# Who makes the low halves of the weights: VectorE alone up to the first squared-ReLU MLP, VectorE and GpSimd from there on

## The chip, the core and the metric

The kernel runs on one core of a Trainium2 chip. The metric is the device time of one execution in microseconds (us). TensorE, VectorE, ScalarE and GpSimd each work through a list of instructions of their own in order, SyncE issues the loads, and semaphores hold them together. In the profile they are called PE (its weight loads PEld), DVE, ACT, POOL and SP.

## What is computed

Two transformer blocks in float32, batch 1, 512 tokens, width 1024, one after the other. What matters here is the order of the weight products:

```
first block
  proj = rmsnorm(x) @ w_in                 # q, k, v of two attentions, forget gates
  forgetting attention, 8 heads; stick-breaking attention, 8 heads
  x += concat(rmsnorm(fox_o), rmsnorm(sb_o)) @ w_out
  x += memory attention(rmsnorm(x), rmsnorm(mem); w_mq, w_mkv) @ w_mo
  u  = depthwise causal conv, width 3 (rmsnorm(x) @ w_up)     # 2 x 2816 columns
  x += (silu(gate) * val) @ w_down
second block
  z = gelu(rmsnorm(x) @ a_w_in);  u, v = split(z);  v = layernorm(v)
  x += (u * (W_s v + b)) @ a_w_out          # gated unit, 8 groups
  x += square(relu(rmsnorm(x) @ w1_0)) @ w2_0
  x += latent attention(rmsnorm(x)) @ b_w_o
  x += square(relu(rmsnorm(x) @ w1_1)) @ w2_1
  out = rmsnorm(x)
```

## The kernel before

Every large product is made of three matmuls in a reduced float32 format: both operands are split into a high half and a low half (the rest), and high x high, high x low and low x high are summed in a bank of TensorE's output memory, PSUM (split_sum, L374 to L385).

**The weight stream.** The weights come in 168 chunks of 128 x 2048 elements (1 MB), in the order in which TensorE uses them. weight_stream (L60) lists them; an item "tiles" in that list is no chunk, it only counts output tiles. 90 chunks stand ahead of the first call of mlp (L118), 78 from there on. raw, w_hi and w_lo have two slots each, so chunk c goes where chunk c-2 was. A chunk is split in PIECES = 2 halves j. SyncE loads chunk c into raw when chunk c-2 has been split (L308 to L312). ScalarE makes both halves of w_hi, a copy that rounds (split_high, L1447 to L1458), when TensorE has finished with chunk c-2. For w_lo = raw - w_hi, VectorE makes half 0 (split_low, L779 to L788), GpSimd makes half 1 (L350 to L353). TensorE waits for both before it uses the chunk (wait_chunk, L361).

**Where the halves stand in the order.** GpSimd has nothing else to do after its constants, so its half starts when ScalarE's second half is ready. VectorE's half is a place in its program: split_low() stands between the things that it does at each stage, and ScalarE has split_high() in the matching places. In the attentions the two halves of a chunk are split at two different steps of the loop (FOX_PIECES, SB_PIECES, MEM_PIECES, L268 and L269). VectorE's call for half 1 there issues nothing.

**What goes on around it.** TensorE writes output tiles to four banks in turn (next_bank, L365) and takes a bank again when VectorE has emptied the tile four before it (take, L790). VectorE empties back projections with L846, x += bank. In the conv MLP of the first block the unit is a granule of 256 up columns for gate and for value: TensorE does two chunks of up projection (by_feature), and one chunk of back projection (back, L419) of the granule before. VectorE takes four up tiles (L1109) with split_low after the second and the fourth, then runs gated_and_back (L1144): the convolution with L1120 and L1126, the products L1136, the low halves g_lo (L802), and between them the eight L846, and split_low at the end. Granules 1 to 10 run so; granule 0 has no back tiles beside it. In the gated unit VectorE does per group the biases (L1243), two takes (L1248), two products (L1256), two g_lo (L802) and eight L846, then split_low.

Of the kernel before, what the change touches and what calls it, by code (L numbers as in the profile page):

```python
# [35 lines left out]
PIECES = 2  # L36
# [23 lines left out]
def weight_stream(w):  # L60

    def columns(name, first, n=COLS, tiles=2):
        v = w[name].rearrange("(k p) n -> p k n", p=P)
        def parts(raw):
            return [(raw.rearrange("p (k n) -> p k n", n=COLS)[:, :, 0:n], v[:, :, first:first + n])]
        return SLOT, tiles, parts, max(n, P)

    def rows(name, granule):
        v = w[name].rearrange("(k p) n -> p k n", p=P)
        def parts(raw):  # L70
            return [(raw.rearrange("p (k n) -> p k n", k=2), v[:, 2 * granule:2 * granule + 2, :])]
        return SLOT, KT, parts, 0

    def k_rope(raw):
        v = w["kv_w_a_2"].rearrange("(k p) n -> p k n", p=P)
        d = raw.rearrange("p (k n) -> p k n", n=COLS)
        a, b = v[:, :, KV_LORA:KV_LORA + 32], v[:, :, KV_LORA + 32:KV_LORA + 64]
        return [(d[:, :, 0:32], a), (d[:, :, 32:64], b), (d[:, :, 64:96], b), (d[:, :, 96:128], a)]

    def q_heads(pair):  # L80

        v = w["b_w_q_b_2"].rearrange("(k p) n -> p k n", p=P)
        def parts(raw):
            d = raw[:, 0:3 * 512].rearrange("p (k n) -> p k n", n=512)
            out = []
            for j in range(2):
                at = (2 * pair + j) * (NOPE + ROPE)
                out += [(d[:, :, 256 * j:256 * j + 192], v[:, :, at:at + 192]),
                        (d[:, :, 256 * j + 192:256 * j + 224], v[:, :, at + 160:at + 192]),
                        (d[:, :, 256 * j + 224:256 * j + 256], v[:, :, at + 128:at + 160])]  # L90
            return out
        return 3 * 512, 4, parts, 0

    def kv_heads(c):
        v = w["kv_w_b_2"].rearrange("(k p) n -> p k n", p=P)
        return SLOT, 8, lambda raw: [(raw.rearrange("p (k n) -> p k n", k=2), v[:, :, 1024 * c:1024 * c + 1024])], 0

    def mlp(up, down):
        u = lambda g: columns(up, COLS * g)
        d = lambda g: rows(down, g)  # L100
        return [u(0), u(1)] + [x for i in range(14) for x in (d(i), u(2 + i))] + [d(14), d(15)]

    g = lambda n: columns("w_up", COLS * n)
    v = lambda n: columns("w_up", D_FF + COLS * n)
    d = lambda n: rows("w_down", n)
    w_in = lambda kind, n=2: [columns("w_in", HEADS * HD * kind + COLS * c) for c in range(n)]
    mkv = lambda *cs: [columns("w_mkv", COLS * c, tiles=2 if c < 4 else 1) for c in cs]
    out = [("tiles", KT)] + w_in(0) + [("tiles", KT), columns("w_in", 6 * HEADS * HD, n=HEADS, tiles=1)]
    out += w_in(1) + w_in(2) + mkv(0, 1, 2, 3) + w_in(3) + w_in(4) + w_in(5) + mkv(4, 5, 6)
    out += [rows("w_out", c) for c in range(2)] + mkv(7) + [rows("w_out", c) for c in range(2, 4)]  # L110
    out += [columns("w_mq", COLS * c) for c in range(4)] + [rows("w_mo", c) for c in range(4)]
    out += [g(0), v(0), g(1), v(1)] + [x for i in range(9) for x in (d(i), g(2 + i), v(2 + i))] + [d(9), d(10)]
    gate_v, gate_u = ([columns("a_w_in_2", at + COLS * c) for c in range(8)] for at in (GATE, 0))
    out += gate_v[0:6] + [("tiles", 2)] + gate_v[6:8] + [("tiles", 2)]
    out += gate_u[0:7] + [("tiles", 2)] + gate_u[7:8]
    for c in range(8):
        out += [("tiles", 2)] * (c < 7) + [rows("a_w_out_2", c)]
    out += mlp("w1_0", "w2_0")  # L118
    out += [columns("b_w_q_a_2", 0), columns("b_w_q_a_2", 256, n=128, tiles=1)]
    out += [columns("kv_w_a_2", 0), (SLOT, 1, k_rope, P)]  # L120
    out += [q_heads(p) for p in range(4)] + [kv_heads(c) for c in range(2)]
    out += [rows("b_w_o_2", c) for c in range(4)]
    out += mlp("w1_1", "w2_1")
    return out


def build(nc, w, out):
# [5 lines left out]
    with ExitStack() as ctx:  # L133
# [83 lines left out]
        w_split = sem("w_split")  # L217
# [56 lines left out]

        CHUNKS, ENDS, LOADS = [], [], []
        passed, loads = 0, [0, 0]
        for item in weight_stream(w):
            passed += item[1]
            if item[0] != "tiles":
                loads[len(CHUNKS) % 2] += 16 * len(item[2](raw[:, 0, :]))  # L280
                LOADS.append(loads[len(CHUNKS) % 2])
                CHUNKS.append(item)
                ENDS.append(passed)

        def split_piece(c, j):

# [10 lines left out]
        @block.sync  # L297
        def _(sp):
            x_cols = x_in.rearrange("(t p) n -> p t n", p=P)

            for c, (_, _, parts, _) in enumerate(CHUNKS):
                if c == 1:
                    for q in range(4):
                        sp.dma_start(x_stage[:, :, 256 * q:256 * q + 256], x_cols[:, :, 256 * q:256 * q + 256])\
                          .then_inc(x_loaded[q], 16)
                if c == 2:
                    sp.dma_start(mem_stage, mem_in.rearrange("(t p) n -> p t n", p=P)).then_inc(mem_loaded, 16)
                if c >= 2:  # L308
                    sp.wait_ge(w_split, c - 1)
                    sp.wait_ge(w_split_pool, c - 1)  # L310
                for dst, src in parts(raw[:, c % 2, :]):
                    sp.dma_start(dst, src).then_inc(w_loaded[c % 2], 16)  # L312

            for k in range(4):
                half, t = OUT_PIECES[2 * k]
                sp.wait_ge(out_vector, k + 1)
                sp.wait_ge(out_scalar, k + 1)
                cut = slice(512 * half, 512 * half + 512)
                sp.dma_start(out.rearrange("(t p) n -> p t n", p=P)[:, t:t + 2, cut], out_stage[:, t:t + 2, cut])\
                  .then_inc(stored, 16)  # L320
            sp.wait_ge(stored, 16 * 4)


        @block.gpsimd
        def _(pool):
            def in_turn(n, ins):

                ins.then_inc(consts, 1)
                pool.wait_ge(consts, n)

            G = nc.gpsimd
            in_turn(1, G.memset(ident[:], 0.0))
            in_turn(2, G.memset(ones[:], 1.0))
            in_turn(3, G.memset(causal[:], 0.0))
            in_turn(4, G.memset(strict[:], 0.0))
            in_turn(5, G.memset(chunked[:], 0.0))
            in_turn(6, G.memset(eps_t, EPS))
            in_turn(7, G.memset(one_col, 1.0))
            in_turn(8, G.memset(phase[0:64], float(np.pi / 2)))
            in_turn(9, G.memset(phase[64:96], float(np.pi)))  # L340
            in_turn(10, G.memset(phase[96:128], 0.0))
            in_turn(11, G.memset(chunked[0:64, 64:128], MASKED))
            in_turn(12, G.affine_select(out=ident[:], in_=ident[:], compare_op=ALU.not_equal, fill=1.0, base=0,
                                        pattern=[[-1, P]], channel_multiplier=1))
            in_turn(13, G.affine_select(out=causal[:], in_=causal[:], compare_op=ALU.is_ge, fill=MASKED, base=0,
                                        pattern=[[-1, P]], channel_multiplier=1))
            in_turn(CONSTANTS, G.affine_select(out=strict[:], in_=strict[:], compare_op=ALU.is_gt, fill=MASKED, base=0,
                                               pattern=[[-1, P]], channel_multiplier=1))

            for c in range(len(CHUNKS)):  # L350
                hi, lo, src = split_piece(c, 1)
                pool.wait_ge(w_hi_done, PIECES * c + 2)
                G.tensor_tensor(lo, src, hi.bitcast(F32), ALU.subtract).then_inc(w_split_pool, 1)  # L353
# [3 lines left out]
        def _(pe):  # L357
# [1 line left out]
            unit, group = Count(), Count()  # L359

            def wait_chunk():  # L361
                pe.wait_ge(w_split, chunk.n + 1)
                pe.wait_ge(w_split_pool, chunk.n + 1)

            def next_bank():  # L365
                if tile.n >= 4:
# [397 lines left out]
        def _(dve):  # L764
# [14 lines left out]
            def split_low(pieces=PIECES):  # L779

                for _ in range(pieces):
                    if low_n.n < PIECES * len(CHUNKS):
                        c, j = low_n.n // PIECES, low_n.n % PIECES
                        low_n.n += 1
                        if j == 0:
                            hi, lo, src = split_piece(c, 0)
                            dve.wait_ge(w_hi_done, PIECES * c + 1)
                            V.tensor_tensor(lo, src, hi.bitcast(F32), ALU.subtract).then_inc(w_split, 1)  # L788

            def take(fn):  # L790
# [1034 lines left out]
```

## Time and profile before

| | |
|---|---|
| three timed runs | 2155.72, 2160.51, 2160.49 us; median 2160.49 |
| the profiled execution | 2156.18 us, its span 2154.4 |
| PE busy in the span | 2056.0 us (95%) |
| PEld | 1684.9 us (78%) |
| DVE | 1337.5 us (62%), 1905 instructions |
| ACT | 759.9 us (35%) |
| POOL | 424.9 us (20%), 186 instructions, 168 of them halves of w_lo |
| L353, a half of w_lo on POOL | 168 times, mean 2513 ns |
| L788, a half of w_lo on DVE | 168 times, mean 1322 ns |
| mean granted TensorE clock | 0.992 |

A timeline row gives the start in the span, the duration, the engine, the line of the kernel, the operation, output <- inputs with their shapes, and how many like it were merged; the bracket at its end says how long the engine was idle before it and what ended that. "arena" is a large buffer in SBUF that many stages use; "bank" is PSUM. Records of one engine overlap a little, so the distance from start to start is the price of an instruction among others.

### The profile page before, as it was taken

The page shows a single profiled execution, that of the slowest core. Times are in us where ns is not written, and L with a number is a line of the kernel's source. Part 1 is how long each engine was busy: PE and PEld are TensorE (multiplying, and loading weights), DVE is VectorE, ACT ScalarE, POOL GpSimd, SP SyncE. Part 2 cuts the span into 40 slices and gives each one's busy share as a digit, 9 for nine tenths or more (in the row PEclk, how much of TensorE's full clock was granted, in tenths as well). Part 3 has the DMA queues.
Part 4 walks back from the last instruction along what each step waited for, and adds up shares of the span by engine and source line. Part 5 has one row for each costly group of instructions (what it writes and reads, how often), then busy time and mean ns, then how long its engine had stood idle before and what let it go on. Part 6 is the DMA issues. An engine that isn't in the chain of part 4 may idle for free.

```text
span 2154.4 us, 24700 instructions
## 1 busy us (share of the span) xinstructions
PE 2056.0 (95%) x10045; PEld 1684.9 (78%) x10045; DVE 1337.5 (62%) x1905; ACT 759.9 (35%) x1187; POOL 424.9 (20%) x186
## 2 busy tenths in 40 slices
PE   7999998999999999899998999999999999999998
PEld 5877866878777777699876778888877777888887
DVE  7564487647757565763778864545489667454545
ACT  4353253334433333342322332222252445322223
POOL 2212111201221212112221122222222002122221
PEclk9999999999999999999999999999999999999999
DMA  5212221212222222322322132223233112332321
GB/s 160 79 40 78 78 79 34 96 47 75 95 86 94 83 96 82 114 69 89 98 79 78 59 98 98 98 98 98 98 74 107 40 40 78 98 98 98 98 98 59
DMA packets 138577, 181.39 MB, mean 84 GB/s; under 512 B 14688, under 2 KB 120288, under 8 KB 138464
## 3 DMA queue, kind: packets, MB, share of 16 engines
q1 hardware_dynamic: 136832, 178.30, 25.6%
q8 instruction: 80, 1.31, 0.2%
q10 hardware_dynamic: 1632, 1.51, 0.2%
q14 instruction: 33, 0.27, 0.0%
HBM read 177.70 MB, written 2.10 MB: 83 GB/s over the span
## 4 chain that ended last, share of the span: by engine, by line
PE 78%; DVE 15%; ACT 3%; issue 3%; DMA 0%; DVEq 0%; ACTq 0%
PE bank L382 23%; PE bank L384 23%; PE bank L383 23%; PE bank L503 6%; DVE arena L1120 2%; PE bank L495 2%; ACT w_hi L1457 2%; DVE resid L846 1%; DVE w_lo L788 1%; DVE arena L1126 1%; DVE biases L1243 1%; DVE arena L827 1%; DVE rstd L838 1%; DVE g_lo L802 1%; DVE arena L877 1%
## 5 line engine op out<-in xcount | busy, mean ns | idle before, releaser
L353 POOL TENSOR_TENSOR w_lo<-raw,w_hi 128x1024 fp32r<-128x1024 f32 (+2 forms) x168 | 422.1, 2513 | 1700.6 <-ACT w_hi L1457 1700.6
L382 PE MATMUL bank<-h_hi,w_hi 128*128 128x512 f32 x1340 | 528.9, 395 | 9.0 <-DVE h_lo L802 4.8
L384 PE MATMUL bank<-h_hi,w_lo 128*128 128x512 f32 x1340 | 523.4, 391 | 0.0
L383 PE MATMUL bank<-h_lo,w_hi 128*128 128x512 f32 x1340 | 523.2, 390 | 0.0
L1457 ACT ACTIVATE w_hi<-raw 128x1024 fp32r<-128x1024 f32 (+2 forms) x336 | 333.9, 1037 | 502.3 <-PE bank L384 499.4
L382 PE MATMUL bank<-g_hi,w_hi 128*128 128x512 f32 (+1 forms) x1036 | 409.5, 395 | 42.6 <-DVE resid L846 27.3
L846 DVE TENSOR_TENSOR resid<-bank,resid 128x512 f32<-128x512 f32 x504 | 334.9, 685 | 127.8 <-PE bank L384 127.4
L384 PE MATMUL bank<-g_hi,w_lo 128*128 128x512 f32 (+1 forms) x1036 | 397.0, 383 | 0.0
L383 PE MATMUL bank<-g_lo,w_hi 128*128 128x512 f32 (+1 forms) x1036 | 396.9, 383 | 0.0
L382 PEld LDWEIGHTS bank<-h_hi,w_hi 128*128 128x128 f32 x1340 | 252.9, 189 | 65.5 <-issue 13.2
L383 PEld LDWEIGHTS bank<-h_lo,w_hi 128*128 128x128 f32 x1340 | 253.0, 189 | 53.6 <-issue 1.9
L384 PEld LDWEIGHTS bank<-h_hi,w_lo 128*128 128x128 f32 x1340 | 252.5, 188 | 53.0
L382 PEld LDWEIGHTS bank<-g_hi,w_hi 128*128 128x128 f32 x1036 | 195.0, 188 | 103.0 <-DVE resid L846 47.8
L788 DVE TENSOR_TENSOR w_lo<-raw,w_hi 128x1024 fp32r<-128x1024 f32 (+2 forms) x168 | 222.0, 1322 | 66.5 <-ACT w_hi L1457 66.2
L384 PEld LDWEIGHTS bank<-g_hi,w_lo 128*128 128x128 f32 x1036 | 194.5, 188 | 39.0
L383 PEld LDWEIGHTS bank<-g_lo,w_hi 128*128 128x128 f32 x1036 | 194.9, 188 | 34.6
L503 PE MATMUL bank<-arena 128*128 128x128 f32 (+4 forms) x928 | 184.5, 332 | 7.1 <-ACT arena L1533 3.1
L1279 DVE SCALAR_TENSOR_TENSOR arena<-bank,rstd 128x512 f32<-128x512 f32 x64 | 44.0, 691 | 219.9 <-PE bank L384 219.8
L503 PEld LDWEIGHTS bank<-arena 128*128 128x128 f32 (+1 forms) x928 | 126.5, 173 | 53.5 <-issue 26.4
L1716 ACT ACTIVATE arena<-arena 128x512 f32<-128x512 f32 x64 | 40.4, 631 | 250.0 <-DVE arena L1279 250.0
L382 PE MATMUL bank<-w_hi,h_hi 128*128 128x256 f32 (+1 forms) x400 | 116.1, 290 | 1.2 <-DVE arena L860 1.2
L383 PE MATMUL bank<-w_lo,h_hi 128*128 128x256 f32 (+1 forms) x400 | 115.5, 289 | 0.0
(182 smaller groups left out, 1868.5 us busy)
## 6 DMA issues: line engine op xcount, KB each, us to landing
raw<-w SPq DMA_DIRECT2D x64, 1024.0 KB, 5.2
raw<-w_up SPq DMA_DIRECT2D x22, 1024.0 KB, 5.1
raw<-a_w_in SPq DMA_DIRECT2D x16, 1024.0 KB, 5.3
raw<-w_in SPq DMA_DIRECT2D x12, 1024.0 KB, 5.3
raw<-w_down SPq DMA_DIRECT2D x11, 1024.0 KB, 4.9
raw<-w_mkv SPq DMA_DIRECT2D x8, 1024.0 KB, 5.4
raw<-a_w_out SPq DMA_DIRECT2D x8, 1024.0 KB, 4.9
raw<-w_out SPq DMA_DIRECT2D x4, 1024.0 KB, 4.9
```

What stands on the lines that cost most here:

```text
L353: G.tensor_tensor(lo, src, hi.bitcast(F32), ALU.subtract).then_inc(w_split_pool, 1)
L382: nc.tensor.matmul(dst, a_hi, b_hi, start=(k == 0), stop=False)
L383: nc.tensor.matmul(dst, a_hi, b_lo, start=False, stop=False)
L384: last = nc.tensor.matmul(dst, a_lo, b_hi, start=False, stop=(k == n - 1))
L495: last = nc.tensor.transpose(pt_bank[:, P * k:P * k + P], prob[:, u % 2, P * k:P * k + P], ident[:])
L503: ins = nc.tensor.matmul(dst, a, b, start=first, stop=last)
L788: V.tensor_tensor(lo, src, hi.bitcast(F32), ALU.subtract).then_inc(w_split, 1)
L846: take(lambda b: V.tensor_tensor(x[:, n, :], b[:], x[:, n, :], ALU.add))
L1120: keep_order(V.scalar_tensor_tensor(conv_y[:, j, :], conv_u[:, j, 1:S + 1], w_col("conv_w1", j), conv_y[:, j, :], ALU.mult, ALU.add))
L1279: take(lambda b: V.scalar_tensor_tensor(r_buf[:, j, :], b[:], 0.0, rstd[:, 0, :], ALU.max, ALU.mult))
L1457: A(hi, src, ACT.Copy).then_inc(w_hi_done, 1)
L1716: A(t_buf[:, j, :], r_buf[:, j, :], ACT.Square)
```

## The change

w_lo of the first 90 chunks is made by VectorE alone. weight_stream returns the number of chunks ahead of the first mlp beside the list (NOT_SHARED, 90). For a chunk c below it split_low issues a subtraction for half 0 and one for half 1, each at its own call, and each behind a wait for the same half of w_hi; GpSimd's loop begins at chunk 90. From chunk 90 on all is as before. The waits count accordingly: by_vector(n) and by_pool(n) are the numbers of halves that each of the two has made when n chunks are split, and SyncE and TensorE wait for GpSimd only at chunks that it shares.

```diff
@@ weight_stream
+    not_shared = sum(item[0] != "tiles" for item in out)
     out += mlp("w1_0", "w2_0")
...
-    return out
+    return out, not_shared
@@ build
-        for item in weight_stream(w):
+        stream, NOT_SHARED = weight_stream(w)
+        for item in stream:
...
+        SHARED = [c >= NOT_SHARED for c in range(len(CHUNKS))]
+
+        def by_vector(chunks):
+            return PIECES * chunks - sum(SHARED[:chunks])
+
+        def by_pool(chunks):
+            return sum(SHARED[:chunks])
@@ sync
-                    sp.wait_ge(w_split, c - 1)
-                    sp.wait_ge(w_split_pool, c - 1)
+                    sp.wait_ge(w_split, by_vector(c - 1))
+                    if SHARED[c - 2]:
+                        sp.wait_ge(w_split_pool, by_pool(c - 1))
@@ gpsimd
-            for c in range(len(CHUNKS)):
+            for c in range(NOT_SHARED, len(CHUNKS)):
@@ tensor
-                pe.wait_ge(w_split, chunk.n + 1)
-                pe.wait_ge(w_split_pool, chunk.n + 1)
+                pe.wait_ge(w_split, by_vector(chunk.n + 1))
+                if SHARED[chunk.n]:
+                    pe.wait_ge(w_split_pool, by_pool(chunk.n + 1))
@@ vector, split_low
-                        if j == 0:
-                            hi, lo, src = split_piece(c, 0)
-                            dve.wait_ge(w_hi_done, PIECES * c + 1)
+                        if j == 0 or not SHARED[c]:
+                            hi, lo, src = split_piece(c, j)
+                            dve.wait_ge(w_hi_done, PIECES * c + j + 1)
                             V.tensor_tensor(lo, src, hi.bitcast(F32), ALU.subtract).then_inc(w_split, 1)
```

## Rows read from the trace of the kernel before

**Rows 1.** The page, part 1: busy us, share of the span, instructions.
```profile
PE 2056.0 (95%) x10045; PEld 1684.9 (78%) x10045; DVE 1337.5 (62%) x1905; ACT 759.9 (35%) x1187; POOL 424.9 (20%) x186
```
**Rows 2.** The page, part 4: shares of the chain that ended last, by engine.
```profile
PE 78%; DVE 15%; ACT 3%; issue 3%; DMA 0%; DVEq 0%; ACTq 0%
```
**Rows 3.** Windows of L353: stretch, its length, POOL busy (count), clock, DMA share, GB/s.
```profile
0.00:1216.00 1216.00, 230.37 (x90) 0.99 0.26 83
```
**Rows 4.** Waits of PE, 0 to 1216: us in total, times, longest.
```profile
PE bank L382 <- DVE resid L846: 25.2, 47, 1.1
```
**Rows 5.** Timelines of DVE, POOL and PE, one granule of the first MLP.
```profile
605.91 1.23 DVE L788 TENSOR_TENSOR w_lo<-raw,w_hi 128x1024 fp32r<-128x1024 f32 x1 [0.46 <-ACT w_hi L1457]
607.05 3.56 DVE L1120 SCALAR_TENSOR_TENSOR arena<-arena,vec 128x512 f32<-128x512 f32 x2
611.13 1.40 DVE L1120 SCALAR_TENSOR_TENSOR arena<-arena,vec 128x512 f32<-128x512 f32 x2
...
621.70 3.20 DVE L788 TENSOR_TENSOR w_lo<-raw,w_hi 128x1024 fp32r<-128x1024 f32 x1
629.61 0.69 DVE L1109 TENSOR_TENSOR arena<-bank,rstd 128x512 f32<-128x512 f32 x1 [4.11 <-PE bank L384]
...
641.64 1.23 DVE L788 TENSOR_TENSOR w_lo<-raw,w_hi 128x1024 fp32r<-128x1024 f32 x1 [0.46 <-ACT w_hi L1457]
...
606.90 2.50 POOL L353 TENSOR_TENSOR w_lo<-raw,w_hi 128x1024 fp32r<-128x1024 f32 x1 [8.38 <-ACT w_hi L1457]
...
611.26 0.50 PE L382 MATMUL bank<-g_hi,w_hi 128*128 128x512 f32 x1 [1.11 <-DVE resid L846]
```
**Rows 6.** Gated unit, one group: DVE, L1243 by itself (ns min/median/max), and PE.
```profile
1128.59 2.75 DVE L1243 SCALAR_TENSOR_TENSOR biases<-arena,vec 128x128 f32<-128x128 f32 x2
1131.37 1.41 DVE L1248 SCALAR_TENSOR_TENSOR arena<-bank,vec,biases 128x512 f32<-128x512 f32 x2
...
L1243 DVE SCALAR_TENSOR_TENSOR biases<-arena,vec x16: 337/1412/2487, 1100.3 to 1208.8; 128x128 f32<-128x128 f32 x16
...
1132.18 0.50 PE L382 MATMUL bank<-g_hi,w_hi 128*128 128x512 f32 x1 [1.40 <-DVE arena L1248]
```
**Rows 7.** Chain in order of time (start, us, what), and PE's timeline: sums of squares.
```profile
22.62 2.21 DVE arena L827
...
922.71 4.43 DVE arena L827
...
933.35 2.07 PE L447 MATMUL bank<-arena,ones 128*128 128x512 f32 x2 [1.64 <-DVE arena L827]
```
**Rows 8.** Timelines of DVE and PE, out projection.
```profile
371.17 2.83 DVE L1012 SCALAR_TENSOR_TENSOR arena<-arena,vec,rstd 128x512 f32<-128x512 f32 x1
...
376.12 0.77 PE L382 MATMUL bank<-h_hi,w_hi 128*128 128x512 f32 x1 [4.79 <-DVE h_lo L802]
```
**Rows 9.** Timelines of DVE and PE, second attention, a middle step and its end.
```profile
316.37 0.69 DVE L880 TENSOR_TENSOR arena<-arena 128x512 f32<-128x512 f32 x1
...
347.79 2.65 DVE L880 TENSOR_TENSOR arena<-arena 128x512 f32<-128x512 f32 x1
...
350.50 1.11 PE L495 MATMUL bank<-ident,arena 128*128 128x128 f32 x4 [2.42 <-DVE arena L880]
```
**Rows 10.** Timeline of PE, the start: transposes of mem.
```profile
48.21 1.97 PE L461 MATMUL bank<-ident,arena 128*128 128x128 f32 x8 [1.02 <-DVE arena L974]
```
**Rows 11.** Timelines of DVE and ACT, memory attention, third step.
```profile
451.31 0.42 DVE L900 TENSOR_REDUCE small<-bank 128x1 f32<-128x256 f32 x1
...
451.44 1.05 ACT L1457 ACTIVATE w_hi<-raw 128x1024 fp32r<-128x1024 f32 x1
```
**Rows 12.** Timeline of DVE, first attention, L885 at two steps.
```profile
138.71 1.51 DVE L885 TENSOR_SCALAR arena<-arena,small 128x384 f32<-128x384 f32 x1
...
149.25 0.42 DVE L885 TENSOR_SCALAR arena<-arena,small 128x384 f32<-128x384 f32 x1
```

## The prediction

> **What bounds the kernel now.** I read the page first. TensorE's matmul records cover 95% of the span and VectorE's 62% [rows 1]. The chain that ended last is 78% TensorE and 15% VectorE [rows 2]. So the kernel runs at TensorE's pace with places where VectorE holds it up, and a change on VectorE and GpSimd is worth what it does at those places. The second view is the waits of the stretch that the change touches, 0 to 1216 us, where all 90 chunks concerned are split [rows 3]. There TensorE waits longest in total for L846, the addition that empties a bank: 25.2 us in 47 waits [rows 4]. By the code, 40 of them are four in each of the ten gated stretches of the first MLP, 7 are in the gated unit behind it.
>
> The third view is the timeline of one such stretch, engine by engine [rows 5]. VectorE makes its half of w_lo at 605.91. GpSimd starts the other half at 606.90. The next VectorE work, two L1120, takes 3.56 us, while the next pair of the same line, at 611.13, takes 1.40. The three rows together say what the excess is: 606.90 + 2.50 is 609.40, and 607.05 + 3.56 less one L1120 (0.7) is 609.9, so the first L1120 ends just behind GpSimd. It stood still while GpSimd worked. At 621.70 it is VectorE's own w_lo half that takes 3.20 us in place of 1.23. VectorE operations that have one operand in PSUM are not stretched so (L1248 below, L846). TensorE's four banks are full by then, and it stands still 1.11 us before the matmul at 611.26, which waits for L846, which waits behind the L1120 pair.
>
> **The price of the moved work.** A second half on VectorE costs what the first does: 1.23 us by its record, 1.14 from its start to the next start, 607.05 less 605.91 [rows 5]. It must wait for ScalarE's second w_hi half. GpSimd waits for the same thing today and started at 606.90, before VectorE would turn to it at 607.05, so this wait is over. For each chunk the change therefore adds 1.14 us to VectorE and takes away a standstill of about 2.1 us where one followed, and nothing where none did. It adds no DMA. The loads of raw are issued by SyncE when both halves are made: about 1.2 us earlier in the stretch above (607.05 + 1.14 = 608.2 against 609.4). I cost that at nothing: VectorE's waits for w_hi here end with ScalarE, not with a load, and an earlier load can only help.
>
> **First MLP, granules 1 to 10.** Removed 3.56 - 1.40 = 2.16, added 1.14: VectorE reaches L846 1.02 us sooner. TensorE stands 1.11 us there, so all 1.02 comes back, and the waits behind it are set by VectorE's own pitch and stay. Ten times: 10.2 us. The other standstill, 3.20 us at 621.70, becomes two halves of 1.14, 0.9 us shorter, but VectorE is idle 4.11 us before 629.61 in any case [rows 5]: nothing. Next late is still VectorE, by its gated operations.
>
> **Gated unit, granules 1 to 7.** The same figure: w_lo at 1127.45, then two L1243 from 1128.59 to the L1248 at 1131.37, 2.78 us [rows 6]. One L1243 that was not held takes 0.337 us, so the pair about 0.59 (two, less the overlap of 0.09). 2.78 - 0.59 - 1.14 = 1.05. TensorE stands 1.40 us before 1132.18 for exactly that L1248. Seven times: 7.4 us.
>
> **Sum of squares ahead of the gated unit.** The first L827 takes 4.43 us in the chain, 2.21 when nothing holds it (a slightly shorter case, at 22.62, both 128x2048) [rows 7]; the chain's 0.09 of overlap belongs to it. 4.52 - 2.21 - 1.14 = 1.2 us, below the 1.64 that TensorE waits.
>
> **Out projection.** L1012 at 371.17 takes 2.83 us, with a standstill of 2.1 as above; TensorE waits 4.79 for what follows it [rows 8]. 2.1 - 1.14 = 0.95 us.
>
> **End of the second attention.** L880 takes 2.65 us against 0.69 at 316.37 [rows 9]. 1.96 - 1.14 = 0.8, of which 0.1 goes to ScalarE's second half, which ends 0.1 after VectorE would be ready: 0.7 us. TensorE waits 2.42 there.
>
> **The start, a loss.** VectorE copies query tiles and then mem tiles out of the banks with two w_lo halves between, and TensorE waits for it four times up to 48.21 [rows 10]. The operands of those copies are in PSUM, so nothing stood still and nothing comes back. Added: 0.6 (the half of the narrow forget chunk, 512 wide, an estimate from the 1.14 for 1024) and 1.14, and 0.1 for the first chunk, whose second half goes ahead of the copies of x (bounds 0 and 1.14; the later sum of squares, no longer held, should take up the rest). Loss 1.9 us.
>
> **Memory attention, a loss.** In its third step ScalarE's second half starts at 451.44 and ends at 452.49. VectorE would wait for it ahead of the L900 that it did at 451.31 [rows 11], finish at 453.65, and be 2.3 us late with that L900. ScalarE's exp and the next L885 queue behind. By following the steps one by one I find the next transposes about 0.6 later, an estimate. I take 0.6; the bounds are 0 and 2.3.
>
> **First attention and the rest of the second.** Eight chunks. The second half joins a loop in which VectorE has little rest, but the standstill leaves it: L885 at 138.71 takes 1.51 us against 0.42 at 149.25, an excess of 1.1 [rows 12], against an added 1.14. In the second attention it is 2 against 1.14. I take nothing for the eight, with 0.5 us each way per chunk as bounds, which is 4 us in all. The chunks between stages, where VectorE waits 2 to 4 us for TensorE, are taken at nothing too: that rest is their cover, and without it each would cost 1.14.
>
> **The sum.** 10.2 + 7.4 + 1.2 + 0.95 + 0.7 - 1.9 - 0.6 = 17.95 us. Against its own time, 2156.18 (span 2154.4 and 1.8 around it), this gives 2138.2. The three timed runs lie at two levels, 2155.7 and 2160.5, and their median is 4.3 above the profiled run; from the median the same sum gives 2142.5. I forecast 2140, between them.
>
> The Trainium skill (SBUF — State Buffer, Who interferes with whom) says that a VectorE instruction with two SBUF inputs and a GpSimd instruction that reads SBUF exclude one another for the whole instruction. Taken at its word the L1120 above would stand still for all of 2.50 - 0.15 = 2.35 us; the row shows 2.16. By the page the seventeen granules would give 17 x 0.19 = 3.2 us more. The row decides.
>
> **Rivals.**
> 1. The added work is bare. If the excess of L1120 and L1243 were not GpSimd's doing, say a cost of reading just-written w_lo or arena, it would stay. Then each of the 17 granules loses 1.14 (19.4), the three single places 3.4, the start 1.9, memory attention 0.6: 25.3 us, 2181.5. For it speaks that VectorE is already what TensorE waits for; against it, that the held operations end with GpSimd's and that the second L1120 pair of each granule is short. It decides as soon as less than 1.14 of the 2.16 is given back. Chance 0.04. The Trainium skill (Perfetto Trace Analysis, Optimizing Scalar/DVE Operations) names this side: with a saturated VectorE, giving work to GpSimd may make sense, though it adds that the two share a read port.
> 2. The attention loops pay in full. If each of the 12 chunks split inside a loop costs the 2.3 us of the worst step in [rows 11], that is 27.6 less the 0.6 counted: 2138.2 + 27.0 = 2165.2, slower than before. It decides from 1.5 us a chunk. Against it: in the memory attention the 1.14 falls on idle time at two of three chunks, and in the first attention the standstill of 1.1 leaves. Chance 0.03. A milder form, 0.5 us a chunk, gives 2138.2 + 6 = 2144.2 (2146 between the levels); chance 0.17.
> 3. Only half of what VectorE gains in the granules reaches TensorE, because something else is late next (the w_hi halves on ScalarE, the two g_lo behind). Then 8.8 are missing: 2149 between the levels. Against it: TensorE's own wait, 1.11 and 1.40, is longer than the 1.02 and 1.05. Chance 0.08.
> 4. More than counted: the standstill before 629.61 is worth something after all (10 x 0.9), or TensorE's clock holds where its shorter waits end: 2131. Chance 0.06.
> 5. The change does not do what it says: a boundary that is off by some chunks would leave records of L353 before 1216. The counts of the code (90 items before the first of mlp) and of the trace agree [rows 3], so 0.01; with nothing moved, 2158.
>
> **How the numbers follow.** The forecast, within 3.5 us of 2140, has 0.61; the rest is as above. The range 2133 to 2150 takes in the forecast, the mild form of 2 and most of 3, about 0.85. A measurement of this kernel tells 0.3%, 6.5 us, from no change, so faster means below 2154. The forecast, the mild form, 3 and 4 lie there, 0.92. No change holds 5, 0.01, and slower 1 and 2, 0.07. I move 0.01 from the first to no change, for causes not thought of.
>
> **What would show it.** L353 has 78 records, all behind 1190; L788 has 258. L1120 has no record above 0.8 us and L1243 none above 0.4. The period of the first MLP's granules falls from 35.73 (605.91 to 641.64) to 34.7, and that of the gated unit by 1.05. TensorE's wait at the first held bank falls from 1.11 to about 0.1, and the three behind it stay at 0.26. The start is 1.9 us longer at the 48.21 row. Behind 1216 each stage keeps its length. The prediction is wrong if the L1120 pair behind w_lo stays over 2 us, if a new wait for ScalarE's w_hi appears before L788 in the MLP, or if the attention stages grow by more than 4 us together.

## The result, and the profile after

| | before | changed |
|---|---|---|
| median of the runs | 2158.59 us (2155.72 to 2160.51, 4 runs) | 2139.51 us (2136.2 to 2141.2, 4 runs) |
| profiled execution, its span | 2156.18, 2154.4 us | 2140.0, 2138.2 us |
| ratio | | 0.9911, 95% interval 0.9892 to 0.9929 |

The changed kernel is 19 us faster, 0.9%. Forecast were 2140.0 us and a range from 2133 to 2150. In a second comparison the ratio was 0.9915 (0.9902 to 0.9927).

All lines of the changed kernel stand 11 or 12 further down: L353 is now L364, L788 is L800, L846 is L858, L1120 is L1132, L1243 is L1255, L382 is L394. First its page, part 1 and the engines of the chain, to be laid beside [rows 1] and [rows 2]:

```profile
PE 2057.2 (96%) x10045; PEld 1685.0 (79%) x10045; DVE 1337.2 (63%) x1995; ACT 759.5 (36%) x1187; POOL 194.4 (9%) x96
...
PE 80%; DVE 13%; ACT 3%; issue 3%; DMA 0%; DVEq 0%; ACTq 0%
```

The waits of TensorE up to 1196 us, beside [rows 4]:

```profile
PE bank L394 <- DVE resid L858: 13.3, 36, 0.9
```

GpSimd's halves by windows, beside [rows 3]:

```profile
0.00:1190.00 1190.00, 0.00 (x0) 0.99 0.26 84
1190.00:2138.00 948.00, 191.65 (x78) 1.00 0.27 86
```

VectorE has 90 instructions more and is busy no longer than before: 90 added halves of 1.2 us took the place of about as much time in which its instructions stood still. That is why a share of busy time alone would not have shown the gain. The wait for L858 went from 25.2 us in 47 places to 13.3 in 36. The granule of the first MLP that answers to [rows 5], VectorE and then TensorE:

```profile
605.21 2.36 DVE L800 TENSOR_TENSOR w_lo<-raw,w_hi 128x1024 fp32r<-128x1024 f32 x2 [0.46 <-ACT w_hi L1469]
607.48 1.41 DVE L1132 SCALAR_TENSOR_TENSOR arena<-arena,vec 128x512 f32<-128x512 f32 x2
608.81 0.68 DVE L858 TENSOR_TENSOR resid<-bank,resid 128x512 f32<-128x512 f32 x1
...
627.88 0.69 DVE L1121 TENSOR_TENSOR arena<-bank,rstd 128x512 f32<-128x512 f32 x1 [4.75 <-PE bank L396]
...
611.47 0.50 PE L394 MATMUL bank<-g_hi,w_hi 128*128 128x512 f32 x1 [0.26 <-DVE resid L858]
```

Two halves of w_lo stand where one stood, the pair of L1132 takes 1.41 us, and the wait of 1.11 at the first held bank is down to 0.09 (the matmul at 609.5, not shown); the row at 611.47 is the second bank's, at the 0.26 that it had before. The start behaved as forecast too: TensorE's row at 48.21 [rows 10] begins at 50.04 now, 1.8 us later. The gated unit, to be laid beside [rows 6]:

```profile
1101.30 2.36 DVE L800 TENSOR_TENSOR w_lo<-raw,w_hi 128x1024 fp32r<-128x1024 f32 x2 [0.46 <-ACT w_hi L1469]
1103.58 0.61 DVE L1255 SCALAR_TENSOR_TENSOR biases<-arena,vec 128x128 f32<-128x128 f32 x2
1104.22 1.41 DVE L1260 SCALAR_TENSOR_TENSOR arena<-bank,vec,biases 128x512 f32<-128x512 f32 x2
...
1105.03 0.50 PE L394 MATMUL bank<-g_hi,w_hi 128*128 128x512 f32 x1 [0.39 <-DVE arena L1260]
```

**Where the time came from.** The same instruction can be looked up in both timelines. I took VectorE's reciprocals, which stand at the boundaries of the stages, and for each the start before less the start after. The differences between neighbours give the stages:

| stretch (time before) | predicted | measured |
|---|---|---|
| start, to 81.8 | +1.9 | +2.3 |
| first attention, to 231.9 | 0 | +0.2 |
| second attention, its end, out projection, to 412.6 | -1.65 | -3.0 |
| memory attention, to 501 | +0.6 | +0.8 |
| first MLP, granules 1 to 10 (10 x 1.01) | -10.2 | -10.1 |
| turn and sum of squares, to 1036.7 | -1.2 | +0.4 |
| gated unit: seven groups, 6.9, and 1.2 ahead of them | -7.4 | -8.1 |
| from 1243 to the last normalisation at 2146 | 0 | 0.0 |
| last store | 0 | +1.3 |
| sum | -17.95 | -16.2 |

The two rows around 1036.7 depend on whose instruction is taken. VectorE's reciprocal there lies 9.4 us earlier in the changed kernel, but TensorE's matmuls beside it lie 10.6 us earlier. By TensorE's instructions, the turn and the sum of squares gain 0.7 us and the gated unit 6.9, with nothing ahead of it.

The last store is no effect of the change: from the last normalisation to the end of the span there are 8.1 us in the kernel before, and also in the second run of the changed kernel (e12); in the profiled execution here there are 9.4.

### The profile page after: what moved, and what is told of

It is laid out like the page before. It is cut to its first block, busy times and chain, and to the rows that moved or that the text cites. A ratio compares the mean times of both kernels' runs of the same rounds, so it can differ in the third digit from the quotient of the medians.

```text
span 2138.2 us, 24579 instructions
## 1 busy us (share of the span) xinstructions
PE 2057.2 (96%) x10045; PEld 1685.0 (79%) x10045; DVE 1337.2 (63%) x1995; ACT 759.5 (36%) x1187; POOL 194.4 (9%) x96
## 3 DMA queue, kind: packets, MB, share of 16 engines
q10 hardware_dynamic: 1632, 1.51, 0.2%
## 4 chain that ended last, share of the span: by engine, by line
PE 80%; DVE 13%; ACT 3%; issue 3%; DMA 0%; DVEq 0%; ACTq 0%
PE bank L394 24%; PE bank L395 24%; PE bank L396 24%; PE bank L515 6%; DVE w_lo L800 3%; ACT w_hi L1469 2%; PE bank L507 2%; DVE arena L1138 1%; DVE arena L1132 1%; DVE resid L858 1%; DVE rstd L850 1%; DVE g_lo L814 1%; DVE arena L889 1%; PE bank L459 0%; DVE arena L892 0%
## 5 line engine op out<-in xcount | busy, mean ns | idle before, releaser
L394 PE MATMUL bank<-h_hi,w_hi 128*128 128x512 f32 x1340 | 528.7, 395 | 7.7 <-issue 4.3
L394 PE MATMUL bank<-g_hi,w_hi 128*128 128x512 f32 (+1 forms) x1036 | 410.2, 396 | 25.2 <-DVE resid L858 16.2
L858 DVE TENSOR_TENSOR resid<-bank,resid 128x512 f32<-128x512 f32 x504 | 334.7, 685 | 125.9 <-PE bank L396 125.4
L364 POOL TENSOR_TENSOR w_lo<-raw,w_hi 128x1024 fp32r<-128x1024 f32 (+1 forms) x78 | 191.7, 2457 | 1913.6 <-ACT w_hi L1469 1913.6
L800 DVE TENSOR_TENSOR w_lo<-raw,w_hi 128x1024 fp32r<-128x1024 f32 (+1 forms) x258 | 305.5, 1209 | 73.5 <-ACT w_hi L1469 73.0
L394 PEld LDWEIGHTS bank<-h_hi,w_hi 128*128 128x128 f32 x1340 | 252.9, 189 | 64.5 <-issue 11.6
L394 PEld LDWEIGHTS bank<-g_hi,w_hi 128*128 128x128 f32 x1036 | 195.3, 189 | 86.0 <-DVE resid L858 37.6
L394 PE MATMUL bank<-w_hi,h_hi 128*128 128x256 f32 (+1 forms) x400 | 116.2, 290 | 1.2 <-DVE arena L872 1.1
```

The costliest lines, as they stand in the source:

```text
L394: nc.tensor.matmul(dst, a_hi, b_hi, start=(k == 0), stop=False)
L858: take(lambda b: V.tensor_tensor(x[:, n, :], b[:], x[:, n, :], ALU.add))
```

## Experiments

### One stage at a time

All the kernels of this group are the changed kernel with another list of shared chunks. GpSimd's loop runs over the shared ones.

```diff
-        SHARED = [c >= NOT_SHARED for c in range(len(CHUNKS))]
+        SHARED = [not 33 <= c < 66 for c in range(len(CHUNKS))]     # e1
+        SHARED = [not 66 <= c < 90 for c in range(len(CHUNKS))]     # e2
+        SHARED = [not 33 <= c < 90 for c in range(len(CHUNKS))]     # e3
...
-            for c in range(NOT_SHARED, len(CHUNKS)):
+            for c in [c for c in range(len(CHUNKS)) if SHARED[c]]:
```

> VectorE makes both parts only for the 33 chunks of the first MLP (33 to 65); every other chunk is shared, as before the change. Theory (each shared half stops VectorE for 2.16 us, the second half costs it 1.14 us, and both stand on the path only ahead of the first held bank of a granule): ten granules, 1.01 us each, nothing at the start, in the attentions and in the gated unit: 2158.6 - 10.1 = 2148.5 us, the granule's period 34.72 us and the gated unit's 15.57 us. Rival (GpSimd's share is a load on the whole kernel, so that the gain goes by the number of chunks taken from it, 19.1 us for 90): 33 chunks give 7.0 us, 2151.6 us.

> VectorE makes both parts only for the 24 chunks of the gated unit (66 to 89), the first of which is split at the turn between the MLP and the unit. Theory: seven groups of 0.98 us and about 0.5 us in the sum of squares and the first product behind it: 7.4 us, 2151.2 us; the group's period 14.59 us, the granule's of the MLP 35.73 us. Rival (gain by the number of chunks): 24 of 90 give 5.1 us, 2153.5 us.

> VectorE makes both parts for chunks 33 to 89; the start and the three attentions (chunks 0 to 32) stay shared. In the trace of the changed kernel the chunks up to 32 lose 3.6 us (start 2.3, first attention 0.2, second 0.3, memory attention 0.8) and win 3.3 us (end of the second attention 1.6, turn behind the output projection 1.7), so that they cancel. Theory: 2158.6 - 10.1 - 7.4 = 2141.1 us by the terms, 2139.2 us by what the changed kernel leaves once its first 33 chunks give back 0.3 us; 2140 us. Rival (gain by the number of chunks): 57 of 90 give 12.1 us, 2146.5 us.

Measured, beside a median of 2156.72 us of the kernel before: e1 2145.66 us (ratio 0.9952, 0.9939 to 0.9966), e2 2150.02 (0.9967, 0.9955 to 0.998), e3 2138.93 (0.9916, 0.9903 to 0.993). The savings are 11.1, 6.7 and 17.8 us. By the number of chunks they would have been 7.0, 5.1 and 12.1. The first two add up to the third, so the stages do not share their gain, and each is worth what its loop said, within about 1 us. e3 is as fast as the changed kernel, so no gain or loss of the first 33 chunks together is seen: what the start and the attentions lose, the places at 350 and 376 us give back.

> VectorE makes both parts only for the eleven chunks of the first MLP whose split stands ahead of the convolution (35, 38, and so on to 65); the other two of each granule and everything else stay shared. Theory (of the three standstills of a granule only the one ahead of the convolution is on the path; the one ahead of the gating product is covered by 4.1 us in which VectorE waits for TensorE, the third meets no VectorE work): the whole gain of the MLP, 11 us as with all 33 chunks: ratio 0.995, period 34.72 us. Rival (each of the 33 chunks carries a third of it): 3.7 us, ratio 0.998.

```diff
+        SHARED = [c not in range(35, 66, 3) for c in range(len(CHUNKS))]
```

2148.49 us, ratio 0.9949 (0.9935 to 0.9963), the same ratio as e1's with a third of its chunks; the kernel before lay at 2160 us in this comparison. In the traces TensorE's way through the first MLP is 10.1 us shorter in e9 and 10.2 in e1. VectorE's idle time ahead of the L1121 that follows the second standstill stays at what it was in the kernel before:

```profile
732.94 0.69 DVE L1121 TENSOR_TENSOR arena<-bank,rstd 128x512 f32<-128x512 f32 x1 [4.14 <-PE bank L396]
...
767.65 0.69 DVE L1121 TENSOR_TENSOR arena<-bank,rstd 128x512 f32<-128x512 f32 x1 [4.10 <-PE bank L396]
```

The period is 34.71 us with the other two standstills still there. So the prediction's "nothing" for the 3.20 us half was right: it costs VectorE 2 us a granule and TensorE none.

### The change carried to the end of the kernel

```diff
+        SHARED = [False for c in range(len(CHUNKS))]
```

> VectorE makes both parts of all 168 chunks and GpSimd none. Theory (what counts is where TensorE waits for VectorE or for a half of the weights): behind the gated unit TensorE waits only 1.8 us for a half of GpSimd's, at one place, where VectorE alone would end it about 1.1 us earlier, and the MLPs there have no wait for VectorE in their loops: 2139.5 - 1.1 = 2138.4 us, between 2137 and 2140. Rival (gain by the number of chunks): 168 chunks give 35.7 us, 2122.9 us. Rival (VectorE's added 1.14 us for each of 78 chunks shows once VectorE has other work beside it): anything above 2142 us.

2172.65 us, ratio 1.0069 (1.0056 to 1.0081): 33 us slower than the changed kernel, 16 slower than the one before. All that this kernel does more is to take 78 further halves from GpSimd. I had expected a gain of one. The third case of the expectation holds, and the trace shows why. First the changed kernel in the second MLP, chunk shared (VectorE, then GpSimd):

```profile
1285.62 1.23 DVE L800 TENSOR_TENSOR w_lo<-raw,w_hi 128x1024 fp32r<-128x1024 f32 x1 [0.26 <-ACT w_hi L1469]
1286.76 2.47 DVE L858 TENSOR_TENSOR resid<-bank,resid 128x512 f32<-128x512 f32 x4
...
1286.61 2.50 POOL L364 TENSOR_TENSOR w_lo<-raw,w_hi 128x1024 fp32r<-128x1024 f32 x1 [10.11 <-ACT w_hi L1469]
```

Then e4, the same granule (VectorE and TensorE):

```profile
1292.64 2.36 DVE L800 TENSOR_TENSOR w_lo<-raw,w_hi 128x1024 fp32r<-128x1024 f32 x2 [0.26 <-ACT w_hi L1469]
1294.92 3.13 DVE L858 TENSOR_TENSOR resid<-bank,resid 128x512 f32<-128x512 f32 x5
...
1295.66 0.50 PE L394 MATMUL bank<-g_hi,w_hi 128*128 128x512 f32 x1 [0.47 <-DVE resid L858]
```

What follows VectorE's half here is L858, with one operand in PSUM and one in the state buffer. Four of them run beside GpSimd's half at 0.6 us each: nothing stands still. GpSimd's help costs nothing there, and a second half on VectorE is bare, 1.14 us ahead of a full set of banks. The granule goes from 21.76 us (1263.86 to 1285.62) to 22.53 (1270.11 to 1292.64). By TensorE's instructions this step of 0.77 comes 14 times in each of the two squared-ReLU MLPs, some 22 us in all. Of the other 11 about 5 come at the entry of the first of them, where a wait of 2.0 us has become 3.1 and matmuls of 0.63 us follow it, and most of the rest comes between the two MLPs; they were not taken apart further. Between the reciprocals at 1225.6, 1578.1, 1787.5 and the end e4 falls back by 15.8, 4.8 and 11.1 us. Rival 1 of the prediction gave a price for bare added work. Its reason, that the excess is not GpSimd's doing, does not hold (e5 below), but the bare work is real: it is what the same edit does one stage further on. What decides is which VectorE instruction comes next.

### Block and added work, each by itself

In e5 the changed kernel gets an idle GpSimd operation in nine granules, the same place and shape as its old half, on a region nobody uses. The first of them, at chunk 36, is a fill. TensorE waits for all of them once, at chunk 66 behind the MLP, when they are long done. e6 and e7 change that operation's form. The lines stand a few further down once more: the w_lo halves are L808, the convolution L1140 and the added operation L366.

```diff
@@ gpsimd
+            spare = at(12288, 1024)
+            for n, c in enumerate(range(36, 65)):
+                pool.wait_ge(w_hi_done, PIECES * c + 2)
+                pool.wait_ge(w_spare, n)
+                ... G.tensor_tensor(spare, spare, spare, ALU.subtract) ... .then_inc(w_spare, 1)   # e5
+                ... G.tensor_copy(spare, spare) ...                                                # e6
+                ... G.memset(spare, 0.0) ...                                                       # e7
```

> The changed kernel, and in chunks 36 to 64 (nine granules of the first MLP) GpSimd also runs a 128x1024 subtraction with two inputs in the state buffer on a region that nothing else uses, released by the second high half, just as its own half was. No other engine waits for it and the output stays whole. Theory (what the change takes away is VectorE's standstill beside GpSimd's two-input operation): the first held operation of a granule takes 2.16 us longer, all of it on the path, since the wait there has just gone to nothing: 9 x 2.1 = 19 us more than 2139.5: 2158 us, the granule's period 36.8 us. Rival (TensorE had waited for GpSimd's half, which ends 1.3 us later than VectorE's would, and no engine is held): nothing waits for the added operation, 2139.5 us.

> As the run before, but GpSimd's added operation is a copy of 128x1024 in place, with one input. If any GpSimd operation on the state buffer holds VectorE's two-input ones for its own length, the time goes up by nine times that length, some 10 to 20 us (2150 to 2160 us); if only GpSimd operations with two inputs do, it stays at 2139.5 us.

> As the run before, but GpSimd's added operation only writes: a fill of 128x1024. If writing alone is enough to hold VectorE, the granule grows by the length of the fill (about 1 us by its 128x128 fills of 0.20 us, so up to 9 us in all: up to 2148 us); if reading is what holds it, 2139.5 us.

e5: 2156.93 us (ratio to the kernel before 0.9997, 0.9988 to 1.0007), 17 us more than the changed kernel. e6: 2147.09 (0.9966), 8 more. e7: 2141.08 (0.9925, 0.991 to 0.994), which can't be told from the changed kernel. The three granules, each VectorE's two halves and GpSimd's operation; first e5:

```profile
755.39 4.06 DVE L808 TENSOR_TENSOR w_lo<-raw,w_hi 128x1024 fp32r<-128x1024 f32 x2 [0.46 <-ACT w_hi L1477]
759.38 1.41 DVE L1140 SCALAR_TENSOR_TENSOR arena<-arena,vec 128x512 f32<-128x512 f32 x2
...
756.38 1.99 POOL L366 TENSOR_TENSOR arena<-arena 128x1024 f32<-128x1024 f32 x1 [8.89 <-ACT w_hi L1477]
```

e6:

```profile
748.11 3.20 DVE L808 TENSOR_TENSOR w_lo<-raw,w_hi 128x1024 fp32r<-128x1024 f32 x2 [0.46 <-ACT w_hi L1477]
...
749.08 1.16 POOL L366 COPY arena<-arena 128x1024 f32<-128x1024 f32 x1 [9.73 <-ACT w_hi L1477]
```

e7:

```profile
741.85 2.36 DVE L808 TENSOR_TENSOR w_lo<-raw,w_hi 128x1024 fp32r<-128x1024 f32 x2 [0.46 <-ACT w_hi L1477]
...
742.82 0.96 POOL L366 MEMSET arena<- 128x1024 f32 x1 [9.91 <-ACT w_hi L1477]
```

The pair of halves takes 2.36 us in the changed kernel, 3.20 beside a copy of 1.16 and 4.06 beside a subtraction of 1.99, so the standstill is 0.84 and 1.70: GpSimd's operation less 0.3, most of which VectorE still works on its first half. Beside a fill of 0.96 it is nothing: the pair takes 2.36 again. Nine times 1.70 is 15.3 and nine times 0.84 is 7.6. Between the reciprocals at 537 and 924 us of the changed kernel e5 falls back by 15.4 us, e6 by 7.6 and e7 by 0.2. I had expected 2.1 a granule for e5, but this operation is shorter than the real half (1.99 against 2.50 us). For e6 I had named two outcomes, 10 to 20 us more or nothing; the 7.6 is the first one with a shorter copy than I had reckoned with. No chunk waits for the added result, so the rival that TensorE had waited for a late half falls. The Trainium skill (SBUF — State Buffer, Who interferes with whom) states just this split: a VectorE instruction with two inputs in the state buffer contends with a GpSimd one that reads it, not with one that only writes. The traces of e6 and e7 agree with it.

e8 is the other half of the pair, more work on VectorE in the kernel before (here the added operation is L794, GpSimd's half L354, the convolution L1127; at chunk 36 it is a fill):

```diff
@@ vector, split_low of the kernel before
                             V.tensor_tensor(lo, src, hi.bitcast(F32), ALU.subtract).then_inc(w_split, 1)
+                        elif 36 <= c < 65:
+                            ... V.tensor_tensor(spare, spare, spare, ALU.subtract) ...
```

> The kernel before, and in chunks 36 to 64 VectorE does a further 128x1024 subtraction on a region that nothing else uses, right behind its own half of each chunk; GpSimd keeps its half. Theory (added VectorE work ahead of the first held bank stands on the path besides the block): 9 x 1.14 = 10.3 us more than 2156.7: 2167 us. If GpSimd's block meets the added operation instead of the convolution's first one, it is only moved, so the sum stays the same. Rival (VectorE, at 62% of the span, has room for it): 2156.7 us.

2168.59 us, ratio 1.0057 (1.0042 to 1.0072), 11.9 us more. Between the reciprocals ahead of the first MLP and behind it, it is 10.8, 1.2 for each of nine granules. The block only moved to the added operation:

```profile
757.28 3.43 DVE L794 TENSOR_TENSOR arena<-arena 128x1024 f32<-128x1024 f32 x1
760.63 1.40 DVE L1127 SCALAR_TENSOR_TENSOR arena<-arena,vec 128x512 f32<-128x512 f32 x2
...
757.13 2.49 POOL L354 TENSOR_TENSOR w_lo<-raw,w_hi 128x1024 fp32r<-128x1024 f32 x1 [8.39 <-ACT w_hi L1464]
```

So e5 and e8 show the two terms separately: the block costs its length less 0.3 us, the added half 1.2 us (the period goes from 35.73 to 36.93), and the gain of the change is their difference.

### Choosing the chunks

> VectorE makes both parts only where the traces show that its standstill beside GpSimd, or the wait for GpSimd's half, is on the path: chunks 22 to 24 (end of the second attention, output projection), 33 to 65 (first MLP), 67 to 89 (gated unit without its first chunk) and 126 (the one chunk behind on whose GpSimd half TensorE waits, 1.8 us). Against the changed kernel it gives back 2.3 us at the start, 0.5 in the first two attentions, 0.8 in the memory attention, 1.4 at the turn to the gated unit, and wins 0.7 at chunk 126: 5.7 us: 2139.5 - 5.7 = 2133.8 us, ratio 0.9885 to the kernel before. Rival (the added halves at these places are hidden as the prediction had it for the attentions, and the terms of the trace are other noise): no faster than the changed kernel, ratio 0.991.

> As the run before, with one chunk in three of the first MLP (35, 38 and so on to 65) in place of all 33. Theory: the same time as the run before within 1 us, since the other two standstills of a granule are not on the path. Rival (they are): 7 us slower than the run before.

> The changed kernel as it is, as a yardstick on the same chip for the three runs before: ratio 0.991 to the kernel before, 2139.5 us.

Beside 2139.91 us (ratio 0.9915) for the changed kernel on the same chip, e10 gave 2137.64 us (0.9902, 0.9888 to 0.9915) and e11 2137.93 (0.9906, 0.9893 to 0.9919). By the medians they are 2 us better than the changed kernel, and the intervals overlap: faster than the changed kernel is likely, not shown. That one chunk in three is enough in the first MLP is shown again. The 5.7 us that I expected did not come. By the same landmarks e10 against e12 has at its last normalisation 3.4 us, and the sum fails at chunk 126. (The 1.4 us counted for the turn came, as 1.6, but through the clock, see below.) e10 at chunk 126, TensorE:

```profile
1597.67 0.47 PE L394 MATMUL bank<-h_hi,w_hi 128*128 128x512 f32 x1 [0.86 <-issue]
1609.36 0.47 PE L394 MATMUL bank<-h_hi,w_hi 128*128 128x512 f32 x1 [3.24 <-DVE arena L873]
```

and the changed kernel:

```profile
1603.32 0.47 PE L394 MATMUL bank<-h_hi,w_hi 128*128 128x512 f32 x1 [1.81 <-POOL w_lo L364]
1613.18 0.47 PE L394 MATMUL bank<-h_hi,w_hi 128*128 128x512 f32 x1 [1.43 <-DVE arena L873]
```

The wait for GpSimd's half shortens by 0.95 us, but VectorE makes the half ahead of the rotary products, everything behind it on VectorE is 0.9 later, and TensorE, which got ahead, waits 3.24 there instead of 1.43. After this longer wait its clock is at half speed for a part of the time (0.86 and 0.71 granted in 1607 to 1615 us, 1.00 in the changed kernel's 1611 to 1619). In all it costs about 2.5 us in e10 and in e11, where 0.7 were to be gained. A version without chunk 126 was not run; from these numbers it would be near 2135 us, an estimate (2137.6 less 2.5).

## Why the prediction was right

**What bounds the kernel** and **the price of the moved work** hold. L1132 has no record above 0.747 us and L1255 none above 0.349, L364 has 78 and L800 258. The block went with GpSimd's work (changed kernel) and came back with it (e5); the added half is 1.14 to 1.2 us wherever it is bare (e4, e8).

**First MLP and gated unit**, 17.6 of the 17.95 us: 10.2 predicted and 10.1 measured, 7.4 and 6.9. e1 and e2 give them one by one. TensorE's first wait in a gated group went from 1.40 to 0.39, 1.01 of the 1.05 counted; the second, 0.86, is 0.90 now. Rival 3, only half reaches TensorE, is refuted for the granules: all of it did.

**Sum of squares and what is around it**: the term was 1.2, and TensorE got half of it. Its wait went from the 1.64 of [rows 7] to 1.02 us:

```profile
924.29 1.10 PE L459 MATMUL bank<-arena,ones 128*128 128x512 f32 x2 [1.02 <-ACT rstd_col L1502]
```

The prediction took the whole of VectorE's gain because it was less than the 1.64. But the wait now ends with ScalarE's rstd_col and no longer with VectorE's L827. This is rival 3, something else late next, at this one place. All ten executions with chunk 67 on VectorE alone wait 1.02 here, and the four with it shared 1.62 to 1.64. Two more things were missed, and both are TensorE's clock. Behind this shorter wait its clock does not fall at once. The kernel before and the changed one:

```profile
931.00:935.00 4.00, 2.36 (x9) 1.46 (x9) 3.93 (x4) 0.84 (x2) 0.00 (x0) 0.79 0.00 0
935.00:939.00 4.00, 4.00 (x19) 3.78 (x18) 3.12 (x6) 0.38 (x1) 0.00 (x0) 0.50 0.01 2
939.00:943.00 4.00, 4.00 (x31) 4.00 (x30) 3.41 (x3) 1.81 (x3) 0.00 (x0) 0.86 0.00 0
```

```profile
922.00:926.00 4.00, 2.98 (x20) 2.20 (x18) 3.56 (x3) 0.84 (x2) 0.00 (x0) 1.00 0.00 0
926.00:930.00 4.00, 4.00 (x22) 4.00 (x22) 3.08 (x6) 0.81 (x2) 0.00 (x0) 0.57 0.00 0
930.00:934.00 4.00, 4.00 (x36) 4.00 (x35) 3.84 (x3) 1.38 (x2) 0.00 (x0) 1.00 0.00 0
```

The columns are the stretch, its length, the busy time of PE, PEld, DVE, ACT and POOL with their counts, the granted clock, DMA share and GB/s. By TensorE's instructions this gave 1.5 us, the second branch of rival 4. It is no fixed price either: of the ten executions with the short wait nine gain 2.1 us in all here on the kernel before and one (e11) 0.8, and of the four with the long wait one (e9) has the full clock too. Ahead of the sum, at the turn, TensorE waits 2.6 to 2.7 us for the low halves g_lo in both kernels. After it the granted clock was 1.00 in the kernel before and 0.79 over 8 us in the changed one, and TensorE's instructions lose 1.6 us there. The eight executions with chunk 66 on VectorE alone all have 0.79 or 0.80. Of the six with it shared, five have 1.00 and one (e9) 0.79. The waits are as long in the one as in the other, so it is not shown that the added half causes the fall; it only goes with it.

**End of the second attention and out projection**: 0.7 and 0.95 were right for the waits (2.42 to 1.74, and 4.79 to 3.68 us). Another 1.5 came from the clock, 1.1 behind the first wait and 0.4 behind the second, and 0.3 was lost in the middle of the second attention. The same kind of windows, of the kernel before and of the changed one:

```profile
350.00:354.00 4.00, 3.50 (x10) 2.57 (x10) 0.44 (x1) 0.60 (x1) 0.00 (x0) 0.50 0.72 232
354.00:358.00 4.00, 4.00 (x17) 3.26 (x17) 1.89 (x3) 1.15 (x2) 0.00 (x0) 0.69 0.08 32
```

```profile
350.00:354.00 4.00, 2.24 (x12) 1.90 (x13) 2.54 (x3) 0.22 (x1) 0.00 (x0) 0.83 0.44 150
354.00:358.00 4.00, 4.00 (x17) 2.81 (x16) 1.38 (x2) 0.38 (x1) 0.00 (x0) 0.74 0.28 113
```

In e12, the same kernel once more, they are 0.60 and 0.54: this part is chance. Over all runs the chunks 22 to 24 on VectorE alone are worth 2.4 us, of which the two waits are 1.8 and for the rest no cause but the clock was found (in six of the eight executions below the rest of the second attention is alone too): from 234 to 412 us six executions with them shared lose 2.2 to 3.0 us on the changed kernel, mean 2.7; the eight with them alone lie between -1.0 and +2.4, mean 0.3.

**The start**: 1.9 predicted, 1.8 at TensorE's row of 48.21, 2.3 in the profiled pair up to 82 us. Eight executions with these chunks shared lie 1.7 us ahead of the changed kernel at 82 us (1.0 to 2.6), six with them alone 0.3: 1.5 us. Added work without a block is a plain loss, as said.

**Memory attention**: 0.6 predicted, an estimate. It costs 0.81, in every one of eight executions with chunks 29 to 31 shared against six with them alone. **First attention**: 0.17 in place of 0, by the same comparison. Rival 2 is refuted in both forms, though each of its terms has its sign. Rival 4 named two causes: the standstill ahead of 629.61 is worth nothing (e9 against e1), while the clock did hold behind one shorter wait. Rival 5 falls with the counts, 78 and 258 records.

The sum was 17.95, and at the last normalisation 17.4 had arrived. The clock moved at three places, +1.5, +1.5 and -1.6, which is 1.4 us in all and was in no term. What the terms stand for gave 16.0, because the sum of squares, the gated unit and the losses at the start and in the attentions were each some tenths worse than counted. So the mechanism held, and the closeness of the number, 2140.0 for 2139.5, is partly luck: the clock made up most of what was missing, and the forecast was a middle between two levels of the kernel before.

## What to carry to other kernels

Before an elementwise operation is shared with GpSimd, or taken back, look at the VectorE instruction that will run beside it. If it reads two operands from the state buffer, GpSimd's help stops it for nearly all of GpSimd's operation (here 2.16 of 2.50 us, for a saving of 1.14). If one operand is in PSUM, the help is free, and taking it back is all cost (here 0.77 us a granule, 33 us over the whole kernel). Two operands are not the only case: the L885 of [rows 12] reads one array and a column of factors, and it was held too: 1.51 against 0.42 us, from 138.71 to 140.22, while GpSimd's half ran from 137.64 to 140.01. Price each place by what TensorE waits for there, and then share by place rather than by stage: eleven chunks of 33 carried the whole gain of the first MLP.

## What the runs showed of the hardware

- A copy of GpSimd with one input (1.16 us) holds VectorE's two-input operation as its subtraction does; a fill that only writes (0.96 us) doesn't.
- It is the engine that comes second that stands still, mostly VectorE here. But GpSimd is held as well when it is second. In the kernel before, its half of 128x1024 takes 2.35 us at 452.56, where VectorE is idle as it starts. It takes 2.50 at 606.90, where VectorE's own half has 0.2 us to go, and 3.35 at 23.71, where the first L827 has 1.1 us to go.
- TensorE's clock after a wait of 2 us is not decided by the kernel alone. Behind the same wait in two executions of the changed kernel, the second MLP's first granule, the matmuls of the first execution stay at 0.39 us:

```profile
1244.30 0.50 PE L394 MATMUL bank<-g_hi,w_hi 128*128 128x512 f32 x1 [2.00 <-DVE resid L858]
1244.64 0.40 PE L395 MATMUL bank<-g_lo,w_hi 128*128 128x512 f32 x1
...
1245.59 0.39 PE L396 MATMUL bank<-g_hi,w_lo 128*128 128x512 f32 x1
```

and those of the second (e12) go to 0.63, the lower of the two levels (1.2 GHz in place of 2.4), from the sixth on and for 3.3 us:

```profile
1243.93 0.50 PE L394 MATMUL bank<-g_hi,w_hi 128*128 128x512 f32 x1 [1.99 <-DVE resid L858]
...
1245.26 0.63 PE L396 MATMUL bank<-g_hi,w_lo 128*128 128x512 f32 x1
...
1248.61 0.40 PE L395 MATMUL bank<-g_lo,w_hi 128*128 128x512 f32 x1
```

  That costs 1.6 us, and the kernel has several such waits, so that differences of 2 us want landmarks in the trace rather than medians.
